# Letting the third expert's weight load wait for the first two gathers of token rows

## The reference, cut to what matters

```python
eid = g_sel[:, None] * EXPERTS_PER_GROUP + top_i        # the token's two experts, inside its best group
comb = one_hot(eid, 32) * top_p * p_sel                 # their gates
for e in range(N_EXPERTS):                              # w_gate, w_up: 1024x256; w_down: 256x1024
    hdn = jax.nn.silu(xt @ w_gate[e]) * (xt @ w_up[e])
    y = y + comb[:, e:e + 1] * (hdn @ w_down[e])
```

## Time and profile before

| | before |
|---|---|
| time, median of 3 runs (lowest, highest) | 1054.77 us (1054.36, 1057.62) |
| the profiled execution's own time | 1052.6 us |
| its span | 1050.8 us |
| PE busy | 909.5 us, 87% |
| DVE busy | 607.8 us, 58% |
| ACT busy | 500.9 us, 48% |
| POOL busy | 235.7 us, 22% |
| DMA | 202.33 MB in all, 193 GB/s over the span |

### The profile page before, as it was taken

One profiled execution on the slowest core, in us unless ns is written; L12 is line 12 of the kernel. 1 busy time (PEld: TensorE's weight loads), 2 busy tenths in 40 slices (PEclk: granted clock), 3 DMA queues, 4 the chain that ended last, 5 costly groups with the idle time before them and its releaser, 6 DMA issues. The chain is left out here.

```text
span 1050.8 us, 14271 instructions
## 1 busy us (share of the span) xinstructions
PE 909.5 (87%) x4955; PEld 716.5 (68%) x4955; DVE 607.8 (58%) x1037; ACT 500.9 (48%) x861; POOL 235.7 (22%) x300
## 2 busy tenths in 40 slices
PE   4899999999999999958969999499999999999700
PEld 3799887887788778835658665377777777777400
DVE  4504432352326332757555326778999899889457
ACT  4523434334433434344312111558888888888312
POOL 1102322222322322323222211211011110100075
PEclk9999999999999999979989998689999999999955
DMA  8123123222131113270253433989999999999685
GB/s 258 39 84 96 63 71 91 75 86 72 57 108 54 46 33 102 76 252 11 57 179 120 155 106 124 359 321 387 388 395 390 393 387 386 394 397 355 250 288 200
DMA packets 90859, 202.33 MB, mean 193 GB/s; under 512 B 11839, under 2 KB 53631, under 8 KB 82598
## 3 DMA queue, kind: packets, MB, share of 16 engines
q1 hardware_dynamic: 80302, 168.40, 45.1%
q0 software_dynamic: 5984, 17.18, 4.8%
q10 hardware_dynamic: 4504, 15.85, 4.0%
HBM read 167.00 MB, written 38.41 MB: 195 GB/s over the span
## 5 line engine op out<-in xcount | busy, mean ns | idle before, releaser
L993 PE MATMUL pj<-n_hi,w_hi 128*128 128x350 f32 (+1 forms) x576 | 198.5, 345 | 3.6 <-DVE n_lo L1313 3.6
L993 PE MATMUL pj<-n_lo,w_hi 128*128 128x350 f32 (+1 forms) x576 | 188.3, 327 | 0.0
L993 PE MATMUL pj<-n_hi,w_lo 128*128 128x350 f32 (+1 forms) x576 | 187.5, 325 | 0.0
L1896 DVE TENSOR_TENSOR e_lo<-e_raw,e_hig 128x2048 fp32r<-128x2048 f32 x64 | 145.9, 2282 | 0.0
L993 PEld LDWEIGHTS pj<-n_hi,w_hi 128*128 128x128 f32 x576 | 109.4, 190 | 32.4 <-issue 30.6
L1275 DVE CUSTOM_DVE_ANT_0 sc<-pj,strip 128x512 f32<-128x512 f32 (+5 forms) x120 | 61.0, 544 | 118.9 <-PE pj L1059 77.4
L1892 ACT ACTIVATE e_hig<-e_raw 128x2048 fp32r<-128x2048 f32 x64 | 122.5, 1918 | 8.0 <-DMA e_raw<-in_w_up 7.6
L993 PEld LDWEIGHTS pj<-n_lo,w_hi 128*128 128x128 f32 x576 | 109.8, 191 | 0.6
L993 PEld LDWEIGHTS pj<-n_hi,w_lo 128*128 128x128 f32 x576 | 109.7, 190 | 0.7 <-issue 0.6
L1944 PE MATMUL pj<-e_hig,xT_hi 128*96 128x512 f32 x256 | 105.3, 411 | 0.0
L1944 PE MATMUL pj<-e_hig,xT_lo 128*96 128x512 f32 x256 | 101.8, 398 | 0.0
(11 more groups left out here) (267 smaller groups left out, 1629.1 us busy)
## 6 DMA issues: line engine op xcount, KB each, us to landing
e_raw<-in_w_up SPq DMA_DIRECT2D x32, 1024.0 KB, 15.2
e_raw<-in_w_gate SPq DMA_DIRECT2D x32, 1024.0 KB, 17.7
e_raw<-in_w_down SPq DMA_DIRECT2D x32, 1024.0 KB, 19.8
w_raw<-in_w_in SPq DMA_DIRECT2D x24, 512.0 KB, 4.1
expert_rows<-yo ACTq DMA_DIRECT2D x32, 384.0 KB, 7.9
expert_rows<-logits SPq DMA_DIRECT2D x22, 384.0 KB, 4.6
wo_raw<-in_w_out SPq DMA_DIRECT2D x8, 512.0 KB, 5.0
k_page<-in_cache_k SPq DMA_DIRECT2D x16, 256.0 KB, 3.8
```

The lines of the kernel that those rows point to most:

```text
L993: ins = pe.matmul(pj[g % 2][:, 0:tn], ws[w][:, P * k:P * (k + 1)], x[:, k, t0:t0 + tn], start=(m == 0), stop=(m == 23))
L1896: eng.tensor_tensor(e_lo[r][:, q, :], e_raw[r][:, q, :], e_hi(par, q).bitcast(F32), ALU.subtract).then_inc(s_lo[q], 1)
```

## The change

The three pieces of expert 2 are no longer issued ahead of the waits; they are issued after them, right before those of expert 3. The waits themselves stay. No other engine's list is changed.

```diff
         def sp_m(sp):
             sp.wait_ge(s_dm, 2 * NT)
-            for q in (1, 0, 2):
-                load_piece(sp, 2, q, 2, 0, 2)
             sp.wait_ge(s_lge, NT)
             sp.wait_ge(s_hsq, NT)
             for r in range(2):
                 sp.wait_ge(s_xg[r], 16)
-            for q in (1, 0, 2):
-                load_piece(sp, 3, q, 3, 0, 3)
+            for e in (2, 3):
+                for q in (1, 0, 2):
+                    load_piece(sp, e, q, e, 0, e)
             for n in range(NE):
                 if n + RD < NE:
                     for q in (1, 0):
```

## The result

| | before | changed |
|---|---|---|
| median (lowest, highest), us | 1053.52 (1051.27, 1057.62), 8 runs | 1058.17 (1054.94, 1060.52), 8 runs |
| ratio, 95% interval | 1 | 1.004 (1.0026 to 1.0053) |
| span of the profiled execution | 1050.8 | 1057.5 |

A forecast was written before the change was run, and what follows sets the result against it. The prediction took PE as the bound, DMA half a microsecond behind at the expert stage's end. With the start gained lost, 2.4 - 0.5 + 0.1 gave +2.0 us on 1054.77: 1056.8 us, 8 in 10 within 1052.5 to 1060.0.

The forecast's parts named there:

- Gain of the gathers: Start of expert stage: without expert 2's pieces beside it, first gather takes 4.3 us; PE starts at most 3.3 us sooner.
- Rival A: First gathers: not helped by moving the pieces, so no gain at the start; +4.8 us, 1059.6 us, chance 0.20.
- No early stall: Start of expert stage: expert 3's up piece lands at 694.6 us, before ACT wants it at 698.3.
- The lag L: Weight pieces after the gathers: the DMA stream stays 2.4 us behind, bounds 0.6 and 5.5 us.
- upper bound of 5.5: Most the DMA stream could lag: 8.1 us for 3.15 MB at 392, less 2.9 us earlier issue, with 0.3 regained.
- Where it surfaces: Late expert stage: ring runs dry eight or nine experts before the present end, then DMA pace; stage ends 1.9 us later.
- the lead: PE's early start at expert 0, 3.3 us, forecast to be lost in full by the end of the expert stage.
- The slack of 0.5 us: Near expert 26: PE takes `hT_lo` 0.5 us after DVE ends it, which absorbs 0.5 us of late landings.
- rival D: Expert stage: PE's short waits lower its granted clock in the last ten experts; some 20 us, about 1077, chance 0.03.
- Short gaps seem harmless: Expert stage, 722 to 957 us: PE's clock stays at 1.00, as only lasting idleness throttles it.
- range of 8 in 10: Whole kernel: 1052.5 to 1060.0 us, leaving out the clock rival and the outer ends of two others.
- The sum: Whole kernel: 2.4 us late, less 0.5 slack, plus 0.1 stalls, gives +2.0 us on 1054.77, so 1056.8 us.

The follow-up runs named there:

- e8_four_gathers: Changed kernel with the six pieces of experts 2 and 3 waiting for four gathers instead of two; 1061.24 us, ratio 1.0055 to the kernel before.
- e7_up_early: Kernel before with expert 2's gate and down pieces moved behind the two gathers, its up piece still early; 1055.73 us, ratio 1.0017.
- e10_bytes_after: Changed kernel loading only half the down piece from expert 8 on, ACT and DVE work kept; 1051.44 us, ratio 0.9983 to the kernel before.
- e9_bytes_before: Kernel before loading only half the down piece from expert 8 on, ACT and DVE work kept; 1051.33 us, ratio 0.9984.
- e1: Kernel before with only expert 2's down piece moved behind the two gathers, its up and gate pieces still early; 1054.40 us, ratio 1.0010.
- e2: Kernel before with expert 3's three pieces also issued without waiting for the gathers; 1055.32 us, ratio 1.0019.
- e4: Changed kernel with its six pieces reordered: up and gate of experts 2 and 3, then both down pieces; 1058.99 us, ratio 1.0050 to the kernel before.
- e11: Kernel before with expert 2's down piece moved late, it and expert 3's pieces waiting for the first gather only; 1053.20 us, ratio 0.9998.
- e6: Changed kernel loading and rounding only half the down piece from expert 8 on; 1051.16 us, ratio 0.9963 to the kernel before.
- e3: Kernel before with expert 2's pieces moved behind the last logits and norm waits, still ahead of the gather wait; 1053.42 us, ratio 0.9999.
- e5: Kernel before loading and rounding only half the down piece from expert 8 on; 1049.69 us, ratio 0.9954.

## Why the prediction was right in kind and short in size

**Gain of the gathers: right.** Forecast 4.3 us for the first and PE's start 3.3 us sooner; measured 4.4 and 3.4. Rival A (gathers not helped) is out.

**"No early stall": wrong.** I had expert 3's up piece at 694.6, from 2.52 us per piece at 416 GB/s and 1 us for the gathers between them. It landed at 702.2, ACT waited 5.9 us, PE 3.2, and one down product ran at half clock, 2.7 us more. The wrong number is the rate. 416 GB/s was read from 655:675, where there is next to nothing but weight pieces; six pieces issued right behind the gathers share the engines with the gathers of experts 2 to 5 and later ones. The stretch had 324 GB/s.

**The lag L: mis-sized, 2.4 us against 6.1 by the bytes and 6.6 by the landing near 943 us.** This is the term of the sum that failed, and it is the same fault. I made the account in bytes, at 400 GB/s, where the engines' time was what ran out: over 686 to 714 us they were full (1.02) at 356, and so moved 1.2 MB less than I had, 3.1 us. An account in shares, made now and with the result known, comes nearer. Before, 684:686 and 686:714 leave 2 x 0.42 + 28 x 0.05 = 2.2 us of engine time unused. The 3.15 MB need 8.0 us at 392, full flow starts 3.0 us sooner, and the lag is 8.0 - 2.2 = 5.8 us when the 3.0 are taken as spent on the gathers, as e8_four_gathers says they are. My upper bound of 5.5 looks near by luck: its own terms, 8.1 less 2.9 and less 0.3 regained, give 4.9, and the low rate is in none of them.

**Where it surfaces: right in the outcome, wrong in the form.** That the lead is lost in full because the stream of pieces is late is what e7_up_early and e10_bytes_after show. But the stage does not go over to the DMA engines' pace some eight experts before its end: SP's issues of up pieces, which follow PE's slots, come 9.37 us apart over most of the stage to its end, 10.2 and 9.9 us apart at 805.64 to 825.69, and 12.9, 10.4 and 12.1 us apart (835.05 to 847.95, 876.04 to 886.44, 914.54 to 926.66) over slots 15, 19 and 23, the ones with routing work on DVE and PE; before these three were 10.4 to 10.5 us. The lateness turns into lost time in a few slots and not evenly.

**The slack of 0.5 us: wrong.** It absorbed nothing. The stretch grew by 7.1 us where the landings were 6.6 late. The late pieces push ACT's and DVE's lists back, and where DVE has routing work as well PE waits for `place_x` (3.1 us instead of 1.0). The kernel before already pays 1.7 us of DMA time by e9_bytes_before, so there seems to have been no slack to spend; the one instruction pair that I had looked at was not the tightest.

**The clock, rival D: its mechanism was there, at a small part of its price.** I had listed a granted clock under 1.00 between 722 and 957 us as a sign of D, and it is 0.99. It fell twice in the changed kernel: behind the wait of 3.16 us that I hadn't forecast (2.66 us), and behind the wait of 1.24 us in slot 15 (some 1.6 us). "Short gaps seem harmless" was wrong. After 722 us it fell once in each of seven kernels (the changed one, e1, e2, e4, e7, e8, e11), in slot 15 or 23, behind a wait of 1.24 to 1.58 us for `place_x`; three more such waits of 1.34 to 1.58 us in these kernels were not followed by a fall. Nor were waits of 1.90 and 2.29 us for `hT_lo` near 710 us (e8, e10), while one of 2.00 us there was (e6): the length of the wait alone doesn't decide it. In before, e3, e5, e6, e9 and e10 it stays at full from 722 us on. The Trainium skill's page "TensorE: Matmul & The Clock Gate" (section "Part 1: The HAM clock gate") has the throttled clock as the default state, which activity releases and idleness brings back. The traces agree in that each fall in the expert stage stands behind a wait of PE. I had taken from the page that only lasting idleness does it; a single wait of 1.24 us was enough, and the measurement decides.

**The range: right partly by luck.** The +4.2 us lie outside the forecast's own +0.5 to +3.5. They lie in the range of 8 in 10 because that was opened towards rival A's price of +4.8, and A did not happen. "Within 0.3%" had a chance of 0.60 and "slower by over 0.3%" 0.32; it was 0.4%.

**The sum.** In absolute time the lead drops out, as forecast, and what is left is the lag and the slack: 6.6 + 0.5 = 7.1 us for the profiled pair where I had 2.4 - 0.5 + 0.1 = 2.0. Over all runs it is 4.2 us. Why this pair is further apart than the medians stays open; that the clock fell behind the early wait in the changed kernel's execution (2.66 us), and not in those of e8_four_gathers and e10_bytes_after, may be part of it. The step of the prediction that failed is thus L: 3.15 MB left undone were taken as refilled to 2.4 us of lag, and the runs showed 6.1 to 6.6.

## What to carry to other kernels

Where DMA is the second limit of a later stage, an early transfer is a loan of engine time: a wait ahead of it is paid for some 130 to 250 us later, in a few slots that have no room, out of sight of the place where it was put. Account for such a stretch in the DMA engines' busy share and not in bytes at the best rate seen, since gathers beside large pieces filled the engines at 324 GB/s where pieces alone had 416. And let the small urgent transfers go first only as far as the ring will be full again before it matters: here the wait is worth about 2 us ahead of the fourth expert's pieces and costs 4 ahead of the third's.

## What the runs showed of the hardware that I had not expected

- Six pieces of 1 MB queued beside gathers of up to 96 rows of 4 KB: 324 GB/s at a share of 1.02. Started after four of the gathers had landed: 382 GB/s at the same share, and the fourth piece lands at the same time although issued 3.8 us later. The Trainium skill's page "DMA: Bandwidth & Descriptors" (section "Queues, rings and completion order") says that each DMA engine takes turns between its queues, packet by packet. The runs agree in so far as neither queue simply stands behind the other; a gather took 4.4 us alone, 7.9 beside the last two pieces of expert 2, and 9.6 in e2_all_early beside five pieces. How a packet of one queue waits for another's is shown by no run here.
- A wait of PE of 1.24 us was followed by the lower granted clock (0.50 in 842 to 844 us). Of ten waits for `place_x` of 1.24 to 1.58 us in seven kernels seven were followed by it and three were not, and one of 2.29 us for `hT_lo` was not either.
- The same routing work before the first gather ended at 673.64 to 679.21 us in thirteen profiled executions of kernels that compute alike up to there, a spread larger than the effect of the change.
